# Expert sums freed one PSUM bank at a time, the first routing ahead of the last chunk's heads, projections one per sixteen gathers

## What is computed

```
h2 = rmsnorm(x, norm2_w) * (1 + sc2) + sh2
q  = (h2 @ wq) per head, normalised;  s1 = q1 @ k1.T;  s2 = q2 @ k2.T     # 8 heads, 128 keys each
v1, i1 = top_k(s1, 16);  v2, i2 = top_k(s2, 16)
sv, si = top_k(v1[:, None] + v2[None, :], 16)                             # 16 experts per head
expert = i1[si // 16] * 128 + i2[si % 16];  g = softmax(sv)
act = gelu(sum(u[expert] * h2));  out += (g * act) * v[expert]            # 8 x 16 experts per token
y = rmsnorm(x + g2 * out, final_norm_w)
```

## Time and profile before

| | |
|---|---|
| median of 3 runs | 3297.12 us (3294.46 to 3301.82) |
| the profiled execution | 3296.16 us, span 3294.3 us |
| mean granted TensorE clock | 0.677 of full speed |
| PE busy | 2306.9 us (70%) |
| DVE busy | 2219.6 us (67%) |
| ACT busy | 2000.6 us (61%) |
| POOL busy | 1215.7 us (37%) |
| queue q0, the gathers | 1113.16 MB, 82.5% of 16 engines |
| chain that ended last | DMA 49%, PE 24%, ACT 10%, DVE 8%, issue 5% |

### The profile page before, as it was taken

The page is one execution under the profiler, slowest core; times in us unless marked ns, Lnnn a source line. Parts: engine busy times, 40 slices in busy tenths (PEclk is TensorE's granted clock), DMA queues, the critical chain, the costliest instruction groups (busy, mean ns, idle before and its releaser), DMA issues.

```text
span 3294.3 us, 46115 instructions
## 1 busy us (share of the span) xinstructions
PE 2306.9 (70%) x15134; PEld 1144.3 (35%) x15134; DVE 2219.6 (67%) x5518; ACT 2000.6 (61%) x6402; POOL 1215.7 (37%) x1118
## 2 busy tenths in 40 slices
PE   7999987988668666666666666666666666666544
PEld 5665464333234333333333233223333332232110
DVE  5687256877667767666766676667666766676645
ACT  3332055777666666666666666666666666666655
POOL 0000102344434444444444444444434444443433
PEclk9999997899656556555655565556556655565555
DMA  7232327999999999999999999999999999999998
GB/s 285 87 104 76 81 72 289 390 392 395 405 385 420 420 420 405 420 420 420 395 420 421 419 399 420 420 420 394 420 420 420 395 420 420 420 397 419 421 421 344
DMA packets 184164, 1195.13 MB, mean 363 GB/s; under 512 B 22122, under 2 KB 32906, under 8 KB 44530
## 3 DMA queue, kind: packets, MB, share of 16 engines
q0 software_dynamic: 154240, 1113.16, 82.5%
q1 hardware_dynamic: 29684, 79.02, 6.8%
HBM read 1182.83 MB, written 9.25 MB: 362 GB/s over the span
## 4 chain that ended last, share of the span: by engine, by line
DMA 49%; PE 24%; ACT 10%; DVE 8%; issue 5%; POOL 3%; SPq 1%; DVEq 0%; POOLq 0%; ACTq 0%
DMA r_w<-in_peer_uv,gidx 21%; DMA r_qk<-in_peer_uv,gidx 12%; DMA r_yT<-in_peer_uv,gidx 11%; PE ps L777 6%; PE ps L1030 5%; PE ps L834 3%; PE ps L966 3%; DMA r_vo<-in_peer_uv,gidx 3%; PE ps L926 2%; PE ps L1017 2%; DVE r_w L1971 2%; ACT mixc L1375 2%; POOL r_vo L681 2%; ACT mixc L1374 1%; DVE r_qk L1971 1%
## 5 line engine op out<-in xcount | busy, mean ns | idle before, releaser
L1371 ACT ACTIVATE mixc<-mixc 128x1 f32<-128x1 f32 x1056 | 212.4, 201 | 797.6 <-DVE r_qk L1971 212.0
L681 POOL DMA_INDIRECT r_vo<-in_peer_uv,gidx x273 | 337.9, 1238 | 647.4 <-PE ps L1030 591.1
L1030 PE MATMUL ps<-r_qk 128*32 128x256 f32 x2192 | 273.1, 587 | 374.9 <-ACT r_qk L1379 334.2
L681 POOL DMA_INDIRECT r_qk<-in_peer_uv,gidx x274 | 284.3, 1038 | 413.7 <-PE ps L1030 371.8
L1375 ACT ACTIVATE mixc<-mixc 128x1 f32<-128x1 f32 x1056 | 409.2, 388 | 35.2
L1030 PE MATMUL ps<-r_w,r_qk 128*32 128x256 f32 x1880 | 245.2, 614 | 250.1 <-ACT r_qk L1379 236.8
L681 POOL DMA_INDIRECT r_yT<-in_peer_uv,gidx x274 | 314.6, 1148 | 255.1 <-PE ps L1030 200.6
L1374 ACT ACTIVATE mixc<-mixc 128x1 f32<-128x1 f32 x1056 | 395.1, 374 | 1.0
L1379 ACT ACTIVATE r_qk<-prm,mixc 128x32 f32<-128x32 f32 x1056 | 340.3, 322 | 34.3
L681 POOL DMA_INDIRECT r_w<-in_peer_uv,gidx x235 | 245.4, 1044 | 276.3 <-PE ps L1030 258.2
L1030 PE MATMUL ps<-r_yT,r_qk 128*32 128x256 f32 x2192 | 230.7, 530 | 131.0 <-ACT r_qk L1379 116.4
(11 more groups left out here) (331 smaller groups left out, 4297.1 us busy)
## 6 DMA issues: line engine op xcount, KB each, us to landing
r_w<-in_ada_w SPq DMA_DIRECT2D x18, 1024.0 KB, 5.4
r_w<-in_w_lin SPq DMA_DIRECT2D x16, 512.0 KB, 8.1
r_w<-in_peer_wq SPq DMA_DIRECT2D x6, 1024.0 KB, 24.2
r_hT<-in_peer_wq SPq DMA_DIRECT2D x6, 1024.0 KB, 21.8
r_yT<-in_peer_uv,gidx POOLq DMA_INDIRECT x274
r_qk<-in_peer_uv,gidx POOLq DMA_INDIRECT x274
r_vo<-in_peer_uv,gidx POOLq DMA_INDIRECT x273
r_vo<-in_x_prompt SPq DMA_DIRECT2D x8, 512.0 KB, 7.0
```

The costliest lines, as they stand in the source:

```text
L681: pool.indirect_dma_start(ring[i], None, table, bass.IndirectOffsetOnAxis(gidx_t[:, t % 2, h, c:c + 1], 0)).then_inc(e_ld[i], 16)
L1030: mm = nc.tensor.matmul(ps[c * DEC:(c + 1) * DEC, q // 2, (q % 2) * QC:(q % 2 + 1) * QC], diag[:, s % 4, :], row[:, D + c * QC:D + (c + 1) ...
L1371: wch.mark(nc.scalar.activation(sq[:, i:i + 1], d, ACT.Square, scale=GELU_C ** 0.5 / TANH_K))
```

## The change

The sums of a tile are taken one bank at a time: `final_sum` becomes `final_half(t, i)`, and `final_square` becomes `final_squares(t, i)`; for tiles 1 to 7 bank 0's half is done in slots 101 and 103 of the tile itself, bank 1's in slots 3 and 5 of the next one. For tile 0 bank 0's half is in slot 1 of tile 1 (slot 129). `acc_free` is a pair of semaphores, one for each bank, and the first `mix` of each bank waits for its own. `sum_squares` moves from slot 6 to slot 8.

The first routing: `scores(0, 0)` go to bank 1 and wait for the fourth `turned_y` instead of `carry(8)`; `query(0, 1)` goes to bank 7. On DVE `route(0)` stands ahead of `inter_heads(7)` and `carry(8)`, and the `gated` calls stand after `carry`. On ACT `query(0, 0)` stands at the head of i = 7, `norm(0)` at its end. On PE `turn_places(0)` stands between the two first replications; `turn_y(4)` moves from the loop into the stream.

The projections begin every 16 slots instead of every 14 (the last at 116 instead of 104), `JOIN` is 128 instead of 118, and the routings 5 to 15 begin at other slots.

```diff
--- before.py
+++ after.py
@@ -32,7 +32,7 @@
 TILE_SLOTS = HEADS * TOPK
 RING = 6
 PLACES = 8
-JOIN = 118
+JOIN = 128
 N_SLOTS = (NT - 1) * TILE_SLOTS + S_STEPS * TOPK
 DQ = 256
 EPS = 1e-6
@@ -45,22 +45,21 @@
 NEG = -1.0e30
 NEG_MAX = -3.0e38
 
-K_ROUTE, K_W, K_FIN = 14, 3, 5
+K_ROUTE, K_W, K_FIN = 14, 3, 6
 QUADS, NG = 4, 16
 QC = 256
 SETS = [((0,), (1,), (2, 3), (4, 5), (6, 7)), ((4, 5), (6, 7), (0, 1, 2, 3))] + [
     ((0, 1, 2, 3), (4, 5, 6, 7))] * (NT - 3) + [((0,), (1,))]
 FAST = (1, 2, 3)
-ROUTE_AT = {1: -7, 2: 5, 3: 11, 4: 18, 5: 30, 6: 44, 7: 58, 8: 72, 9: 86, 10: 100, 11: 118,
-            12: 133, 13: 146, 14: 159, 15: 172}
+ROUTE_AT = {1: -7, 2: 5, 3: 11, 4: 18, 5: 33, 6: 49, 7: 65, 8: 81, 9: 97, 10: 112, 11: 124,
+            12: 141, 13: 152, 14: 163, 15: 174}
 ROUTE_AT.update({m: 184 + 16 * (m - 16) for m in range(16, (NT - 1) * HEADS + S_STEPS)})
-PROJECT_AT = {t: 4 + 14 * (t - 1) for t in range(1, NT)}
-PROJECT_AT[NT - 1] = 104
+PROJECT_AT = {t: 4 + 16 * (t - 1) for t in range(1, NT)}
 TURN_AT = (30, 38)
 PIECES = {0: (0, 0, 2), 1: (0, 2, 4), 2: (0, 4, 6), 3: (0, 6, 7), 4: (0, 7, 8),
-          7: (1, 0, 2), 8: (1, 2, 4), 9: (1, 4, 6), 10: (1, 6, 7), 11: (1, 7, 8)}
+          8: (1, 0, 2), 9: (1, 2, 4), 10: (1, 4, 6), 11: (1, 6, 7), 12: (1, 7, 8)}
 GELU_C = 0.044715
-LAST_Y = {0: NT - 4, 2: NT - 3, 4: NT - 2, 6: NT - 1}
+LAST_Y = {0: 4, 1: 5, 3: 6, 5: 7, 6: 8}
 TANH_K = 0.7978845608028654
 LOG1P = [1.0 / k for k in range(3, 19, 2)]
 
@@ -282,7 +281,8 @@
         idx_x, idx_t, gate_x, gate_t2, gate_ready, x_rep, x_copy, f_sq, f_mm = (sem(n) for n in (
             "idx_x", "idx_t", "gate_x", "gate_t2", "gate_ready", "x_rep", "x_copy", "f_sq", "f_mm"))
         e_ld = [sem(f"e_ld{j}") for j in range(PLACES)]
-        dot_done, dg_ready, v_free, acc_free = (sem(n) for n in ("dot_done", "dg_ready", "v_free", "acc_free"))
+        dot_done, dg_ready, v_free = (sem(n) for n in ("dot_done", "dg_ready", "v_free"))
+        acc_free = [sem(f"acc_free{i}") for i in range(2)]
         s_tr, s_ev = sem("s_tr"), sem("s_ev")
         route_step, w_step, fin_step = sem("route_step"), sem("w_step"), sem("fin_step")
         g2_ld, x1_ld, f_var, f_rt, y_out, y_st = (sem(n) for n in (
@@ -344,7 +344,7 @@
 
         def query_bank(m):
 
-            return 4 if m else 6
+            return {0: 6, 1: 7}.get(m, 4)
 
         def turn_bank(t, j):
 
@@ -352,7 +352,7 @@
 
         def score_bank(m):
 
-            return 5
+            return 5 if m else 1
 
         place, uses, last_use = [], [], []
         free = [(i - RING, i) for i in range(RING)]
@@ -377,6 +377,7 @@
                             slots.append((t, h, q, c, len(builds) - 1, number(t, h)))
         assert len(slots) == N_SLOTS
         first.append(N_SLOTS)
+        replicated = [sum(x[0] <= t for x in builds) for t in range(NT)]
         spans = {}
         for n, x in enumerate(slots):
             spans.setdefault((x[0], x[2] // 2), []).append(n)
@@ -981,7 +982,7 @@
                 pe.wait_ge(q_sb, m + 2)
                 pe.wait_ge(r_cp, m + 1)
                 if m == 0:
-                    pe.wait_ge(c_upd, NT)
+                    pe.wait_ge(y_ev, 4)
                 for c in range(2):
                     q = qts[:, c, :] if t < NT - 1 else qs[c][:, h * P:(h + 1) * P]
                     nc.tensor.matmul(ps[:, score_bank(m), c * P:(c + 1) * P], q, kTt[:, c, :], start=True, stop=True)
@@ -1020,8 +1021,8 @@
 
                 t, h, q, _, _, _ = slots[s]
                 pe.wait_ge(dg_ready, s + 1)
-                if t and s == t * TILE_SLOTS:
-                    pe.wait_ge(acc_free, t)
+                if t and s == spans[t, q // 2][0]:
+                    pe.wait_ge(acc_free[q // 2], t)
                 if s == spans[0, 1][0]:
                     pe.wait_ge(y_ev, NT)
                 row = ring[place[s]]
@@ -1073,18 +1074,19 @@
                     project(0, 1, range(4, KD))
                 if i == 1:
                     turn_y(0)
-                if 5 <= i < NT - 1:
+                if 5 <= i < NT - 2:
                     turn_y(i - 3)
                 if i == 6:
                     query(0, 0, 0)
             pe.wait_ge(n_ev, NT)
             replicate(0, 0)
+            turn_places(0)
             replicate(0, 1)
-            turn_places(0)
             turn_gates(0)
-            pe.wait_ge(nd_done, NT)
+            pe.wait_ge(c_upd, NT)
             query(0, 1, 0)
             scores(0, 1)
+            pe.wait_ge(nd_done, NT)
 
             for s in range(N_SLOTS):
                 t, j = slots[s][0], s - slots[s][0] * TILE_SLOTS
@@ -1115,7 +1117,7 @@
                     turn_y(LAST_Y[s])
                 if t < NT - 2 and j in TURN_AT:
                     turn(t + 1, TURN_AT.index(j), P)
-                if t and j == 6:
+                if t and j == 8:
                     sum_squares(t - 1, 4)
             sum_squares(NT - 1, 1)
 
@@ -1406,6 +1408,8 @@
             for i in range(NT):
                 if i == 2:
                     turned_y(0)
+                if i == 7:
+                    query(0, 0)
                 if i >= 1:
                     numerators(i - 1)
                 if i + 1 < NT:
@@ -1418,13 +1422,11 @@
                 if i == 2:
                     open_gate(7)
                     open_gate(8)
-                if i >= 6:
+                if i in (6, 7):
                     turned_y(i - 4)
                 if i == 6:
                     turned(0, 0, 0, P)
                     turned(0, 1, 0, P)
-                if i == 7:
-                    query(0, 0)
                 if i in (1, 2):
                     head_norms(i - 1)
                     head_roots(i - 1)
@@ -1434,7 +1436,7 @@
                 if i >= 4:
                     head_norms(i - 2)
                     head_roots(i - 2)
-                if i == NT - 1:
+                if i == NT - 2:
                     norm(0)
             numerators(NT - 1)
             copy_rows(0, 0)
@@ -1458,7 +1460,7 @@
                 if s - 1 in LAST_Y:
                     turned_y(LAST_Y[s - 1])
                 for u, at in PROJECT_AT.items():
-                    if s == at + (15 if u < NT - 1 else 9):
+                    if s == at + (16 if u < NT - 1 else 9):
                         x1_norm(u)
                         x1_root(u)
                     if u == NT - 1 and s == at + 16:
@@ -1974,29 +1976,29 @@
             def y_quads(t, nq):
                 return [h2h(t, q // 2)[:, q % 2 * QC:(q % 2 + 1) * QC] for q in range(nq)]
 
-            def final_sum(t, nq):
-                fc.base, fc.n = t * K_FIN, 0
+            def final_half(t, i, nq):
+                if i == 0:
+                    fc.base, fc.n = t * K_FIN, 0
                 n = min(nq, 2)
-                parts = [h2h(t, i)[:, 0:n * QC].rearrange("p (q n) -> p q n", q=n) for i in range((nq + 1) // 2)]
-                dve.wait_ge(v_free, RING + (t * TILE_SLOTS + TILE_SLOTS if nq == 4 else N_SLOTS))
+                a = h2h(t, i)[:, 0:n * QC].rearrange("p (q n) -> p q n", q=n)
+                dve.wait_ge(v_free, RING + spans[t, i][-1] + 1)
+                dve.wait_ge(x_rep, 2 * replicated[t])
                 dve.wait_ge(g2_ld, 192)
-                for i, a in enumerate(parts):
-                    last = V.tensor_tensor(a, ps[:, i, 0:n * QC].rearrange("p (q n) -> p q n", q=n),
-                                           (g2b if nq == 4 else g2s).unsqueeze(1).broadcast_to([P, n, QC]), ALU.mult)
-                last.then_inc(acc_free, 1)
-                dve.wait_ge(acc_free, t + 1)
+                V.tensor_tensor(a, ps[:, i, 0:n * QC].rearrange("p (q n) -> p q n", q=n),
+                                (g2b if nq == 4 else g2s).unsqueeze(1).broadcast_to([P, n, QC]), ALU.mult).then_inc(acc_free[i], 1)
+                dve.wait_ge(acc_free[i], t + 1)
                 dve.wait_ge(x1_ld, t * 64 + 64)
-                for i, a in enumerate(parts):
-                    last = V.tensor_tensor(a, a, x1s[:, 2 * i:2 * i + n], ALU.add)
-                fc.mark(last)
-
-            def final_square(t, nq):
+                fc.mark(V.tensor_tensor(a, a, x1s[:, 2 * i:2 * i + n], ALU.add))
+
+            def final_squares(t, i, nq):
                 fc.need()
-                for q, a in enumerate(y_quads(t, nq)):
+                for q in range(2 * i, min(2 * i + 2, nq)):
+                    a = y_quads(t, nq)[q]
                     last = V.scalar_tensor_tensor(fdump, a, 1.0, a, ALU.mult, ALU.mult, accum_out=fss[:, q:q + 1])
                     if q < nq - 1:
                         fc.link(last)
-                last.then_inc(f_sq, 1)
+                    else:
+                        last.then_inc(f_sq, 1)
 
             def final_variance(t, nq):
                 dve.wait_ge(f_mm, t + 1)
@@ -2005,7 +2007,7 @@
             def final_scale(t, nq):
                 dve.wait_ge(f_rt, t + 1)
                 fc.link(V.reciprocal(frs[:, 0:nq], frs[:, 0:nq]))
```

(32 more changed lines are left out.)

## The result

The changed kernel takes 3308.49 us (median of 6 runs, 3307.22 to 3313.18) against 3296.59 us for the kernel before beside it: a ratio of 1.0036, 95% interval 1.0026 to 1.0045. That is 12 us slower, where 6.5 us faster was forecast, and above the range. Its profiled span is 3306.4 us.

A forecast was written before the change was run, and what follows sets the result against it. Gathers were taken to bound the kernel: their start, their bytes' time and empty DMA time. -13 + 6.5 + 0.5 - 2.5 + 2 = -6.5 us from 3296.16 gave 3289.7, as median 3290.6 us; range 3279 to 3303.

The forecast's parts named there:

- The shortfalls from 1.01 sum to 0.46, times 30 us is 13.8 us of empty DMA.: At the seven tile changes from 1|2 to 7|8, DMA share below 1.01 is empty time; per-bank sums win 13 us.
- the empty time moves instead of going: Rival: work in slots 101 to 103 and tight routings cost half the gain, -6.5 for -13, 3297.1 us; chance 0.15.
- First routing, +6.5: At the start, heads(8) and numerators wait behind the earlier route, unhidden; replication, first dot and first mix come 6.5 us later.
- The rival of an earlier route: At the start, the first mix isn't later, so the start gives -3.7 instead of +6.5: 3280.4 us; chance 0.15.
- One more `turn_y` in the stream, +0.5: One turn of 0.60 to 1.1 us in the stream, where PE is the bound: +0.5, between 0 and 1.1.
- Projection spacing, -2.5: First tile: less PE work per slot and no meeting of ACT's table loads give -2.5 us, bounds 0 and -5.
- The pit at 795: First tile: 2.9 us of empty DMA where ACT's table loads meet; -2.5 taken from it and smaller ones near.
- The change of tile 0 to 1, +2: Slot 129: DVE waits for the later loads of g2 and x1, leaving a 3.6 us hole, +2 against before.
- The rival of a 27 us hole: Slot 129: loads need their 58 us even without gathers beside them, hole 27 us, 3315.6 us; chance 0.15.
- the first term: Sums by bank at the seven tile changes: nothing on PE waits there any more, -13 of 13.8 us empty DMA.

The follow-up runs named there:

- e1_bank: The kernel before with the sums taken per bank and nothing else (tile 0's bank 0 half stays in slot 131): 3297.43 us against 3297.62, ratio 1.0000.
- e12_one: The kernel before plus 32 loads per tile of one 8188-byte row, each one packet on one DMA engine: 3333.32 us against 3298.68, ratio 1.0101.
- e2_route: The kernel before with only the first-routing part (other banks, route ahead of inter_heads and carry, turn_y(4) in the stream): 3304.14 us, ratio 1.0022.
- e6_heads: The kernel before with the first routing early, inter_heads(7) left ahead of route(0), only carry(8) behind it: 3306.38 us, ratio 1.0028.
- e3_space: The kernel before with projections one per sixteen slots, JOIN at 128 and the new routing slots, nothing else: 3302.31 us, ratio 1.0013.
- e5_order: The changed kernel with SP's loads of g2, norm weight and x1 ahead of the wq loads: 3303.67 us against 3299.0 for the kernel before, ratio 1.0017.
- e14_mended: The changed kernel with carry ahead of the first routing, state stores early, and small loads ahead of weight loads: 3293.15 us, ratio 0.9990 against the kernel before.

## Why the prediction was wrong

**The step that failed: "The shortfalls from 1.01 sum to 0.46, times 30 us is 13.8 us of empty DMA."** The mean share over 16 engines was read as time that can be won. It was the lead of some engines over the others, as `e1_bank` (windows full, time unchanged), the landings at the changes (first parts 5.5 to 7.4 us apart, last parts 2.5 to 3.2) and `e12_one` (bytes on one engine cost seven times those spread) show. Measured: 0 (interval about -2.6 to +3.0 us) for -13. The mechanism on PE, DVE and POOL was as forecast, and none of the three sets the pace there. The rival "the empty time moves instead of going" came nearer: about half of the shortfall did move (13.6 us to 7.1). But it left half of the gain standing, and all of it failed to come; and DVE's work in slots 101 to 103 isn't the cause, since the pits stand some 75 us into a tile and slots 96 to 112 keep a share of 1.01.

**First routing, +6.5: right.** PE waited for `inter_heads(7)` as forecast (10.68 us, "some 10"). The chain was 1.2 us later throughout, because the scores were: the first max came at 500.29 (499.1 forecast), the route ended at 509.2 (508.1), `inter_heads(7)` at 510.3 (509.2), the replication began at 514.91 (513.75), first dot 526.8 (525.5), first mix 535.2 (533.9). That is +7.8 in the profile, and +6.5 by the medians of `e2_route`. The rival of an earlier route fell. What the prediction missed is the state stores behind `carry(8)`: in this order they are late together with the head norms, but in `e6_heads`, where the heads come in time, they alone make DVE wait 9.84 us. Asking which DMAs hang on a step that is moved would have found them.

**One more `turn_y` in the stream, +0.5:** slots 0 to 1024 of `e2_route`, which has it, take 0.8 us less than before, so no cost shows above the scatter.

**Projection spacing, -2.5:** the empty time in slots 0 to 128 is 0.8 us less than before in `e3_space` and 4.3 us less in the changed kernel (5.3 to 1.0). In the runs with the old spacing this number itself lies between 2.0 and 6.7 us, so the term is neither shown nor refuted. The pit at 795 is gone (1.00).

**The change of tile 0 to 1, +2: the mechanism right, the size too small.** The wait was 24.41 us for "about 30", covered as said; the hole was forecast at 3.6 us and is 5.8 in the 20 us from 925 (4.8 more empty than before over slots 128 to 152). The next gathers came later than the 4 us assumed: DVE goes on at 932.94, and the 5 us windows have 0.42 from 930, 0.45 from 935, 0.91 from 940 and 0.97 from 945. By the runs it is +4.7 (`e3_space`), and ordering the loads takes it away (`e5_order`, `e14_mended`). The rival of a 27 us hole fell: the loads were issued from 907.04 and DVE went on at 932.94, within 26 us, not 58.

With the first term at 0 the prediction's own sum is 6.5 + 0.5 - 2.5 + 2 = +6.5 us, slower. In the changed kernel's own trace the 12 us are 7.8 (start) + 3.7 (slots 0 to 256) + 0.5 (the six tiles behind). In the 3.7 the empty time of spacing and tile change nearly cancels (-4.3 + 4.8 + 0.3 = +0.8); the 2.8 us of longer packets are in no term of the prediction, and no run here explains them.

## What to carry to other kernels

A DMA share below full in a window is not time that can be won until one knows that the slowest engine is idle too: look at when the 16 parts of a transfer land, not at the mean. Look at GB/s beside the share: full share at a tenth of the rate is no work done, so see which transfer went ahead. In one queue the loads that something waits for next go ahead of the large ones that nobody needs yet; here that one edit gave 4.8 us by the medians on the kernel before (1.7 in its profile) and 6 to 7 us on the changed kernel.

## What the runs showed of the hardware

- The 16 landings of a gather drift apart to 4 to 7.5 us (means of 30 us) under a stream of 1 MB gathers, and come back to 2.2 us in a pause. The Trainium skill ("DMA: Bandwidth & Descriptors", iDMA fabric) remarks, within an explanation that it calls unconfirmed, that a bulk load runs at the pace of its slowest engine; `e12_one` agrees, with 4.5 us per tile for 9.9 us of packets on one engine and 0.6 for the same bytes on all.
- 512-byte packets of a DRAM to DRAM copy took 27 ns each, 8 KB ones 311 ns, 16 KB ones 613 ns: an 8 KB row cut into 16 pieces costs 1.4 times the same row whole.
- For some 11 us behind two stores of 544 packets of 4 bytes and 512 of 512 bytes, 8 KB gather packets took 4 to 4.7 us on the mean, single ones 7.7, instead of 0.31.
